# ScalarE's square-root functions asked for ahead of the norms, sigmoid and silu made from exp in the sparse attention, and the two tiles' norm steps interleaved at three places

## The reference, cut to what matters

```python
def rms_norm(x, g):        # ahead of both parts of each hybrid layer, and at its end
    y = xf * lax.rsqrt(jnp.mean(xf * xf, axis=-1, keepdims=True) + NORM_EPS)
    return (y * g.astype(jnp.float32)).astype(x.dtype)
def layer_norm(x, g, b):   # l0, l1, l2, l3 in the kernel
    mu = jnp.mean(xf, axis=-1, keepdims=True)
    var = jnp.mean(jnp.square(xf - mu), axis=-1, keepdims=True)
    return ((xf - mu) * lax.rsqrt(var + LN_EPS) * g + b).astype(x.dtype)
def compress(k, pe, w1, w2):
    ...
    return jax.nn.silu(blk @ w1) @ w2
gates = jax.nn.sigmoid(g_logits.astype(jnp.float32))   # in nsa_mixer
```

## Time and profile before

| what | value |
|---|---|
| median of 3 runs | 2278.53 us |
| lowest and highest run | 2272.89 and 2286.32 us |
| profiled execution, its own time | 2274.16 us |
| its span | 2272.4 us |
| PE, DVE, ACT busy share of the span | 94%, 70%, 58% |
| granted TensorE clock, mean | 0.976 |

### The profile page before, as it was taken

The page is one execution under the profiler, slowest core; times in us unless marked ns, Lnnn a source line. Parts: engine busy times, 40 slices in busy tenths (PEclk is TensorE's granted clock), DMA queues, the critical chain, the costliest instruction groups (busy, mean ns, idle before and its releaser), DMA issues.

```text
span 2272.4 us, 26136 instructions
## 1 busy us (share of the span) xinstructions
PE 2145.5 (94%) x10090; PEld 1727.6 (76%) x10090; DVE 1596.6 (70%) x1554; ACT 1324.1 (58%) x1378; POOL 20.4 (1%) x32
## 2 busy tenths in 40 slices
PE   8889999989999999998888999999999999999997
PEld 7667887767788788777667888788888877777675
DVE  4965555776555645566755555788888899999997
ACT  5454444645444443445644544576776788887886
POOL 0000000000000000000000000000000000000000
PEclk9989999999999999997899999999999999999998
DMA  7314553431655455432007555788998999999995
GB/s 263 139 47 153 185 185 131 167 121 68 250 183 183 150 185 185 164 138 75 1 19 272 211 207 183 272 341 348 342 363 331 367 362 421 392 421 375 421 389 217
DMA packets 74625, 524.29 MB, mean 231 GB/s; under 512 B 8736, under 2 KB 9184, under 8 KB 12160
## 3 DMA queue, kind: packets, MB, share of 16 engines
q1 hardware_dynamic: 71712, 511.64, 59.2%
q0 software_dynamic: 2784, 10.93, 1.4%
HBM read 521.48 MB, written 1.05 MB: 230 GB/s over the span
## 4 chain that ended last, share of the span: by engine, by line
PE 66%; DVE 19%; ACT 6%; issue 6%; DMA 3%; DVEq 0%; ACTq 0%; SPq 0%; POOLq 0%
PE psum L516 57%; DVE LO L507 10%; ACT HI L499 2%; DMA ring<-in_experts 2%; DVE AR L1556 1%; PE psum L1030 1%; PE psum L2406 1%; PE psum L1025 1%; ACT AR L845 1%; PE psum L2434 1%; PE psum L879 1%; PE psum L816 1%; PE psum L664 1%; PE psum L683 1%; PE psum L1943 1%
## 5 line engine op out<-in xcount | busy, mean ns | idle before, releaser
L507 DVE TENSOR_TENSOR LO<-ring,HI 128x2048 fp32r<-128x2048 f32 x379 | 850.8, 2259 | 398.9 <-ACT HI L499 393.2
L499 ACT ACTIVATE HI<-ring 128x2048 fp32r<-128x2048 f32 x379 | 712.7, 1887 | 350.8 <-PE psum L516 340.3
L516 PE MATMUL psum<-HI,XT 128*128 128x512 f32 (+1 forms) x3152 | 805.2, 394 | 22.4 <-issue 5.7
L516 PEld LDWEIGHTS psum<-HI,XT 128*128 128x128 f32 x3152 | 592.4, 191 | 165.4 <-DVE XT L699 10.9
L516 PE MATMUL psum<-LO,XT 128*128 128x512 f32 (+1 forms) x1856 | 507.2, 395 | 16.6 <-DVE LO L507 14.2
L516 PEld LDWEIGHTS psum<-LO,XT 128*128 128x128 f32 x1856 | 345.4, 190 | 112.5 <-DVE LO L507 44.3
L516 PE MATMUL psum<-HI,HTH 128*128 128x512 f32 x848 | 306.3, 402 | 6.9 <-DVE HTH L1082 6.9
L507 DVE TENSOR_TENSOR LO<-AR,HI 128x2048 fp32r<-128x2048 f32 x112 | 254.9, 2290 | 53.6 <-ACT HI L499 53.0
L499 ACT ACTIVATE HI<-AR 128x2048 fp32r<-128x2048 f32 x112 | 212.7, 1911 | 60.3 <-PE psum L516 57.2
L516 PE MATMUL psum<-LO,HTH 128*128 128x512 f32 x848 | 229.9, 393 | 0.0
L516 PE MATMUL psum<-HI,HTL 128*128 128x512 f32 x568 | 221.5, 390 | 0.0
(11 more groups left out here) (270 smaller groups left out, 1464.8 us busy)
## 6 DMA issues: line engine op xcount, KB each, us to landing
ring<-in_experts SPq DMA_DIRECT2D x224, 1024.0 KB, 6.6
ring<-in_dense SPq DMA_DIRECT2D x149, 1024.0 KB, 4.8
AR<-in_experts SPq DMA_DIRECT2D x112, 1024.0 KB, 6.5
bcs<-in_ln_g POOLq DMA_DIRECT2D x4, 512.0 KB, 4.6
bcs<-in_ln_b POOLq DMA_DIRECT2D x4, 512.0 KB, 5.1
bcs<-in_norm_g POOLq DMA_DIRECT2D x3, 512.0 KB, 3.9
cons<-in_cons POOLq DMA_DIRECT2D x1, 1317.0 KB, 8.0
X<-in_x SPq DMA_DIRECT2D x2, 512.0 KB, 4.0
```

The lines of the kernel that those rows point to most:

```text
L499: e.activation(HI[:, h:h + m], slot(u), ACT.Copy).then_inc(*high.up(u))
L507: e.tensor_tensor(LO[:, h:h + m], slot(u), HI[:, h:h + m].bitcast(F32), ALU.subtract).then_inc(*low.up(u))
L516: ins = e.matmul(out_ap, lhsT=a, rhs=b, start=start and n == 0, stop=stop and n == len(pairs) - 1)
```

## The change

`first_root` is a new ScalarE instruction: the square root of a constant into a spare column. It stands ahead of everything in layer 0, and ahead of the squares of `l1`, `l2` and `l3`. The functions of the norms are cut into their steps. In layer 0 both tiles' squares and sums come ahead of tile 0's split, and TensorE turns tile 1's rows ahead of the first product. In `l2` VectorE splits tile 0 only after tile 1's centred values. In `l3` both tiles' means, sums and centred values come ahead of both tiles' rows. In the sparse attention Sigmoid and Silu become Exp of the negated input on ScalarE, and VectorE adds one, takes the reciprocal and, for Silu, multiplies.

```diff
+        def first_root(e):
+            e.wait_ge(*v_done.of("eps"))
+            e.wait_ge(*a_order.last)
+            e.activation(sm(1, "root"), EPS[:, 0:1], ACT.Sqrt).then_inc(*a_done.up())
...
         def ln_stat(e, name, t):
+            if t == 0 and name != "l0":
+                first_root(e)
+            ln_squares(e, name, t)
+            ln_root(e, name, t)
...
             if l == 0:
-                idle_first(e, 10)
+                idle_first(e, 3)
             turn_rows(e, n1, 0, lambda k: ROWS[:, 0, tile(k)], rows_of(n1, 0), rest=l)
-            if l == 0:
-                idle_first(e, 18)
             def second_rows():
                 turn_rows(e, n1, 1, lambda k: ROWS[:, 1, tile(k)], rows_of(n1, 1), wait=l, rest=l, b=BA[0])
-                if l == 0:
-                    idle_first(e, 4)
-            cols_by_tile(e, ("raw", l, 0), ("qk", l, 0), BOTH, xr, between=second_rows)
+            if l == 0:
+                idle_first(e, 6)
+                second_rows()
+            cols_by_tile(e, ("raw", l, 0), ("qk", l, 0), BOTH, xr, between=second_rows if l else None)
...
+            if l == 0:
+                first_root(e)
             rms_stat(e, n1, 0, x_at)
+            if l == 0:
+                rms_squares(e, n1, 1, x_at)
             cols_hi(e, n1, 0)
             if l:
                 split_hi(e)
-            rms_stat(e, n1, 1, x_at)
+                rms_squares(e, n1, 1, x_at)
+            rms_root(e, n1, 1)
             if l == 0:
                 split_hi(e, AHEAD)
...
-                rms_apply(e, n1, t, ROWS, *vector(n1))
+                if t and l == 0:
+                    rms_rows(e, n1, 1, ROWS, *vector(n1))
+                else:
+                    rms_apply(e, n1, t, ROWS, *vector(n1))
                 if t == 0:
+                    if l == 0:
+                        rms_sum(e, n1, 1)
                     cols_lo(e, n1, 0)
...
-            e.wait_ge(*a_done.of("hid", kind))
+            e.wait_ge(*v_done.of("hid", kind))
...
                 e.activation(GT[:, t, :], banks.get("gates", 2, "turned")[:, t * 48:(t + 1) * 48],
-                             ACT.Sigmoid).then_inc(*(a_bank.up("gates", 2, "turned") if t
+                             ACT.Exp, scale=-1.0).then_inc(*(a_bank.up("gates", 2, "turned") if t
...
-                e.activation(hv, hv, ACT.Silu).then_inc(*a_done.up("hid", kind))
+                e.activation(sm(60, "hid").rearrange("p (g n) -> p g n", g=4), hv, ACT.Exp,
+                             scale=-1.0).then_inc(*a_done.up("hid", kind))
...
+        def one_over_one_more(e, x):
+            e.wait_ge(*v_order.last)
+            e.tensor_scalar(x, x, 1.0, None, ALU.add).then_inc(*v_done.up())
+            e.wait_ge(*v_order.last)
+            e.reciprocal(x, x).then_inc(*v_done.up())
+        def hidden_silu(e, kind):
+            hv = HID.rearrange("p (g n) -> p g n", g=4)[:, :, 0:15]
+            ex = sm(60, "hid")
+            e.wait_ge(*a_done.of("hid", kind))
+            one_over_one_more(e, ex)
+            e.wait_ge(*v_order.last)
+            e.tensor_tensor(hv, hv, ex.rearrange("p (g n) -> p g n", g=4),
+                            ALU.mult).then_inc(*v_done.up("hid", kind))
...
+            def gates():
+                e.wait_ge(*a_bank.of("gates", 2, "turned"))
+                one_over_one_more(e, A(16000, 96))
...
+            steps |= {1: gates, 3: lambda: hidden_silu(e, 0), 9: lambda: hidden_silu(e, 1),
...
-            ln_stat(e, "l3", 0)
-            ln_stat(e, "l3", 1)
+            first_root(e)
+            ln_squares(e, "l3", 0)
+            ln_squares(e, "l3", 1)
+            ln_root(e, "l3", 0)
+            ln_root(e, "l3", 1)
...
-                ln_apply(e, "l2", t, *vector("l2"), *vector("l2b"))
-                if t == 0:
+                ln_mean(e, "l2", t)
+                ln_center(e, t, *vector("l2"))
+                if t:
                     cols_lo(e, "l2", 0)
+                ln_sum(e, "l2", t)
+                ln_rows(e, "l2", t, *vector("l2b"))
             cols_lo(e, "l2", 1)
...
-                ln_apply(e, "l3", t, *vector("l3"), *vector("l3b"))
+                ln_mean(e, "l3", t)
+                if t:
+                    ln_sum(e, "l3", 0)
+                ln_center(e, t, *vector("l3"))
+            for t in range(2):
+                if t == 0:
+                    ln_sum(e, "l3", 1)
+                ln_rows(e, "l3", t, *vector("l3b"))
```

More of the change, by code:

```diff
@@ L702, in cols_lo, with rms_squares @@
                                 ALU.subtract).then_inc(*v_bank.up(name, "cols", t, k0))
+        def first_root(e):
+            e.wait_ge(*v_done.of("eps"))
+            e.wait_ge(*a_order.last)
+            e.activation(sm(1, "root"), EPS[:, 0:1], ACT.Sqrt).then_inc(*a_done.up())
         def rms_stat(e, name, t, x_at):
-            st, mv, r = sm(2, "st", t), sm(2, "mv", t), sm(1, "r", t)
+            rms_squares(e, name, t, x_at)
+            rms_root(e, name, t)
+        def rms_squares(e, name, t, x_at):
+            st = sm(2, "st", t)
             for nh in range(2):
@@ L713, in rms_stat, with rms_root @@
                              accum_out=st[:, nh:nh + 1]).then_inc(*a_done.up(name, "sq", t, nh))
+        def rms_root(e, name, t):
+            mv, r = sm(2, "mv", t), sm(1, "r", t)
             e.wait_ge(*v_done.of(name, "sum", t))
@@ L719, in rms_apply, with rms_sum @@
         def rms_apply(e, name, t, dst, gv, g_at):
-            st, mv, r = sm(2, "st", t), sm(2, "mv", t), sm(1, "r", t)
+            rms_sum(e, name, t)
+            rms_rows(e, name, t, dst, gv, g_at)
+        def rms_sum(e, name, t):
+            st, mv = sm(2, "st", t), sm(2, "mv", t)
             e.wait_ge(*a_done.of(name, "sq", t, 1))
@@ L724, in rms_apply, with rms_rows @@
                             ALU.add).then_inc(*v_done.up(name, "sum", t))
+        def rms_rows(e, name, t, dst, gv, g_at):
+            r = sm(1, "r", t)
             e.wait_ge(*a_done.of(name, "root", t))
@@ L735, in ln_stat, with ln_squares @@
         def ln_stat(e, name, t):
-            ss, mv, r = sm(2, "ss", t), sm(2, "mv", t), sm(1, "r", t)
+            if t == 0 and name != "l0":
+                first_root(e)
+            ln_squares(e, name, t)
+            ln_root(e, name, t)
+        def ln_squares(e, name, t):
+            ss, mv = sm(2, "ss", t), sm(2, "mv", t)
             for nh in range(2):
@@ L741, in ln_stat, with ln_root @@
                              accum_out=ss[:, nh:nh + 1]).then_inc(*a_done.up(name, "sq", t, nh))
+        def ln_root(e, name, t):
+            mv, r = sm(2, "mv", t), sm(1, "r", t)
             e.wait_ge(*v_done.of(name, "sum", t))
@@ L747, in ln_apply, with ln_mean @@
         def ln_apply(e, name, t, gv, g_at, bv, b_at):
-            st, ss, mv, r = sm(2, "st", t), sm(2, "ss", t), sm(2, "mv", t), sm(1, "r", t)
+            ln_mean(e, name, t)
+            ln_center(e, t, gv, g_at)
+            ln_sum(e, name, t)
+            ln_rows(e, name, t, bv, b_at)
+        def ln_mean(e, name, t):
+            st, mv = sm(2, "st", t), sm(2, "mv", t)
             e.wait_ge(*v_order.last)
@@ L753, in ln_apply, with ln_center, ln_sum @@
                             ALU.mult).then_inc(*v_done.up(name, "mean", t))
+        def ln_center(e, t, gv, g_at):
             e.wait_ge(*g_at)
             e.wait_ge(*v_order.last)
-            e.scalar_tensor_tensor(ROWS[:, t, :], X[:, t, :], mv[:, 1:2], gv, ALU.add,
+            e.scalar_tensor_tensor(ROWS[:, t, :], X[:, t, :], sm(2, "mv", t)[:, 1:2], gv, ALU.add,
                                    ALU.mult).then_inc(*v_done.up())
+        def ln_sum(e, name, t):
+            ss, mv = sm(2, "ss", t), sm(2, "mv", t)
             e.wait_ge(*a_done.of(name, "sq", t, 1))
@@ L761, in ln_apply, with ln_rows @@
                             ALU.add).then_inc(*v_done.up(name, "sum", t))
+        def ln_rows(e, name, t, bv, b_at):
+            r = sm(1, "r", t)
             e.wait_ge(*a_done.of(name, "root", t))
@@ L2203, in turn_c_vector @@
             e.reciprocal(l, l).then_inc(*v_done.up())
-            e.wait_ge(*a_bank.of("gates", 2, "turned"))
             e.wait_ge(*v_order.last)
@@ L2313, in sparse_vector @@
             steps = {2 * n: f for n, f in steps.items()}
-            steps |= {12: lambda: weigh_c_vector(e, 0), 14: lambda: turn_c_vector(e, 0),
+            steps |= {1: gates, 3: lambda: hidden_silu(e, 0), 9: lambda: hidden_silu(e, 1),
+                      12: lambda: weigh_c_vector(e, 0), 14: lambda: turn_c_vector(e, 0),
                       18: lambda: gather_c_vector(e, 0), 19: lambda: weigh_c_vector(e, 1),
@@ L2739, in vector_program @@
             e.wait_ge(*v_order.last)
-            e.memset(EPS[:, 1:2], 1e-6).then_inc(*v_done.up())
+            e.memset(EPS[:, 1:2], 1e-6).then_inc(*v_done.up("eps"))
             hybrid_vector(e, 0, lambda t, nh: None)
```

## The result

The changed kernel takes 2263.64 us (median of 13 runs, 2258.96 to 2271.4), the kernel before, run beside it, 2276.24 (13 runs, 2269.47 to 2288.87). The ratio is 0.9941, with an interval from 0.9925 to 0.9957: 13.4 us less, between 9.8 and 17.1. The profiled execution took 2260.03 with a span of 2258.2, which is 14.2 less than the span before. The page shows 22 loads of ScalarE's functions instead of 28. First the chain of waits of the kernel after, which answers to the earlier trace rows: TensorE's share grows by 2 points, ScalarE's and DMA's shrink by 1 each.

A forecast was written before the change was run, and what follows sets the result against it. TensorE holds two thirds of the chain; the change touches where it stands still for unfinished norms. Terms 4.0 + 0.7 + 0.6 + 0 + 1.9 + 2.8 + 2.3 = 12.3 us give 2261.9 or 2266.2, middle 2264, range 2256 to 2272.

The forecast's parts named there:

- start, order and fillers, with banks: Layer 0: tile 1's products start at 20.6 to 21.0 instead of 24.75, 4.0 us, plus 0.7 us from banks.
- banks within it: Layer 0, third unit: its products use long-empty banks, so the 0.73 stop at 31.22 goes; 0.7 us.
- l1: Norm l1: the load at 953.13 goes, but TensorE had only 0.51 us idle there; 0.6 us.
- sparse, keys' path: Sparse attention, keys: product 0.95 us later, absorbed by 1.14 us of TensorE idle at 1061.45; together 0.
- sparse, values: Sparse attention, values: two loads in a row on ScalarE go, the weight split at 1084.16 starts at 1082.25; 1.9 us.
- l2: Norm l2: tile 1's transposes start 2.2 us sooner, plus 0.6 for TensorE not falling to half clock; 2.8 us.
- l3: Norm l3, the end: tile 1's residuals directly follow tile 0's centred values, rows end at 2267.65 instead of 2269.93; 2.3 us.
- The cold TensorE: Rival at the start: fewer fillers delay the full clock, losing 3 to 4 us of 4.7, total 8.5; chance 0.20.
- VectorE's dear work: Rival in sparse attention: reciprocals cost twice the slope, sparse gains +0.5 in all, total 10.5 or less; chance 0.15.
- Loads dearer than their rows: Rival: a drain makes four loads on the path give 1.38 more each, gain 17.8; chance 0.04.
- The loads moved as written: Answers the rival that the root's set lacks Square, each norm loading twice more; gain 7, chance 0.03.
- The half clock did not stay on: Answers the slower rival: TensorE at half clock for most of the first stage, 2290 us; chance 0.03.

The follow-up runs named there:

- p_banks: Kernel before with the PSUM bank count moved on by two ahead of layer 0's second projection group; 2277.52 us, ratio 0.9997.
- a_again: Kernel after, unchanged, profiled a second time; 2260.75 us (4 runs), ratio 0.993 to the kernel before.
- p_start: Kernel before with only the start changed: root load ahead, new order, 3 and 6 fillers; 2271.1 us, ratio 0.996.
- b_again: Kernel before, unchanged, profiled a second time; 2280.23 us, ratio 1.0015.
- p_exp: Kernel before with only the sparse attention changed, exp and VectorE work for sigmoid and silu; 2276.48 us, ratio 0.999.
- a_keysilu: Kernel after with the keys' hidden layer back on ScalarE's Silu, the values' still on exp; 2266.45 us, ratio 0.9944.
- p_order: Kernel before with only the order of l2 and l3 changed, loads left in front of the roots; 2275.22 us, ratio 0.9968.
- p_loads: Kernel before with only the square-root loads ahead (first_root at the start, l1, l2, l3); 2270.45 us, ratio 0.9967.
- a_nofill: Kernel after without any filler products at the start (0 in both places); 2269.99 us, ratio 0.9957 to the kernel before.
- four part kernels: p_loads, p_start, p_exp and p_order, each one part of the change on the kernel before; ratios 0.9967, 0.996, 0.999, 0.9968.
- a_gfirst: Kernel after with norm_g's transfer issued ahead of the second tile of x; 2261.26 us, ratio 0.9929 to the kernel before.

## Why the prediction was right

With fourteen traces, the terms can be read at their own places and averaged over kernels that share the code there. The start goes to the split of VectorE that stands at 38.98 in the kernel before. The sparse part goes from the split at 1047.66 to that at 1084.16 (the earlier trace rows has the latter); all distances are differences of row starts.

| term | predicted | measured | from |
|---|---|---|---|
| start, order and fillers, with banks | 4.7 | 5.4 | 38.6 (4 traces without) less 33.2 (5 traces with the change's start) |
| banks within it | 0.7 | 0.9 | `p_banks` |
| l1 | 0.6 | 0.8 | lead of 5.74 at the residual, 6.56 at the next split |
| sparse, keys' path | 0 | -0.7 | 13.79 to 14.47 at the transposes |
| sparse, values | 1.9 | 1.5 to 1.9 | 9.59 to 8.13, and 7.73 in `a_again`, which like before has full clock there |
| sparse, whole region | 1.9 | 3.6 | 37.7 (6 traces) less 34.1 (6 traces) |
| l2 | 2.8 | 2.4 to 2.7 | 16.99 to 14.61; 2.7 with the work up to the next split |
| l3 | 2.3 | 2.05 | 13.08 to 11.03 |
| sum | 12.3 | about 14 | the ratio gives 13.4 (9.8 to 17.1) |

**The start** is the largest term, and was 0.7 too small. The four traces without the change stand between 38.3 and 39.0, the five with it between 32.8 and 34.1, so the gain is beyond the scatter of either. The scatter has two sources: in the kernels without the change the first product (16.05 to 16.75) goes with the time at which the fillers reach the full rate (9.4 to 11.4), and in the five with it the product starts 6.4 to 6.8 us behind the rows that waited for norm_g. The step that was off is "Tile 0's products took 6.1 us": they take 5.6 (14.34 to 19.90 in `p_start`), since nothing waits for VectorE's low halves any more. The first product at 14.34 instead of 14.5 to 14.9 and the banks' 0.2 add to it. In the first trace norm_g came 1.1 us later than I had it from the earlier trace rows, and hid that.

**The keys' product** comes 1.0 later, priced 0.95; the reciprocals take 0.53 and 0.75, priced 0.51 and 0.73, so the line through the earlier trace rows holds up to 96 columns. The 1.14 us of idle at 1061.45 did take up delay, as I had written, and is gone. What my sum lacked is the clock. TensorE's work from the keys' product to its next free moment takes 4.37 us in the kernel before and 5.18 in the kernel after, and 1.01 + 0.81 - 1.14 gives the 0.68 that is lost. The last scores ahead of the idle ran at the full rate before (timeline of the kernel before):

```profile
1059.67 0.65 PE L816 MATMUL psum<-AR 128*128 128x256 f32 x2
```

The same two take 1.17 in the kernel after (row 1054.73). Nor was the load at 1055.79 off the path. In the kernel before, the keys' rotation on VectorE waited for ScalarE's small copy of weights at 1059.60, behind the exps that this load held up. Without the load that copy is only 0.34 us later behind the split (1053.50 in the kernel after), although the product is 1.01 later, and the turned keys too are only 0.34 later.

**The region** gained more than both its steps. With both hidden layers on Silu, the six traces have 36.3 to 39.6 us; with both on exp, 33.5 to 34.6: no overlap. The windows from the second split to the third show why. First `b_again`, one of the long ones, then `a_again`:

```profile
1072.41:1089.28 16.87, 16.29 (x79) 12.54 (x78) 8.50 (x15) 10.63 (x26) 0.00 (x0) 0.73 0.01 2
```

```profile
1064.37:1076.80 12.43, 10.98 (x72) 8.31 (x70) 9.45 (x18) 8.07 (x23) 0.00 (x0) 0.99 0.02 4
```

In the kernel before at 1.00 this stretch takes 14.29, at 0.99 in `a_again` 12.43: 1.86 of gain at the same clock, which is the predicted 1.9. The rest is clock: three of six Silu traces pay 2.6 more here, the exp traces at most 0.7 (`p_exp`, at 0.86; the first trace of after pays 0.4 at 0.84), and `a_keysilu` (16.53 at a clock of 0.72) pays too. Ahead of it, the exp traces are 0.8 quicker to the second split on the mean (21.3 for 22.1), although the keys' product is later. That too goes with the clock. In the seven traces with the keys on Silu, TensorE has a granted clock of 0.57 to 0.65 from the first split to the transposes, stands idle 1.0 to 1.7 us in front of them, and runs at 0.54 to 0.68 behind them, so that the second split comes 7.2 to 8.9 us later. In the seven with the keys on exp it is 0.50, no idle, then 0.74 to 0.93, and 6.6 to 7.15 us. I had no such term. In clock and idle ahead of the second split the two groups do not overlap in 14 traces (in the whole time from first to second split they do: `p_start`, with Silu, takes 20.95). Behind it their clocks overlap: `before`, `p_order` and `p_loads` have Silu and full clock. Why the keys' path should move the clock was not isolated.

**l2, l3** came out as worked, 0.1 to 0.4 and 0.25 less. At l2, of the 2.38 at the routing 1.94 is the earlier transposes, which I had at 2.2, and 0.44 the clock behind them, which I had at 0.6. My reason for the clock isn't borne out: the idle in front shrank to 1.12 and not below 1 us, and `p_loads` runs these transposes at a granted clock of 1.00 behind an idle of 2.68, `p_exp` at 0.84 behind 2.33, the kernel before at 0.55 behind 2.33. Both places repeat well: in the seven traces that have the change there, the routing is at 14.60 or 14.61 and l3 takes 11.03 or 11.04. At l3 the change orders both roots behind both sums, so tile 0's rows start at 7.65 behind the first residual, where I had 7.55, and the two pairs of rows take 3.38 instead of 3.28. The lesson of `p_order` is that my sum there silently used two gains, which alone are worth 0.8 (order) and 1.1 (load).

**The rivals.** The cold TensorE did not come (products of 0.25 from the first) and is sized by `a_nofill`, 1.4 us. The margin was thin: the passes reach the full rate within 0.3 us of the first product in two of the six traces with three and six fillers, the first of the kernel after among them, and 0.9 to 1.8 us ahead in the other four. VectorE's dear work is refuted by its rows. Loads dearer than their rows: `p_loads` shows 1.14 at l3 for a load of 1.28, and the load starts 0.08 us behind ScalarE's last work there, where I had 0.04. The Trainium skill ("ScalarE: Activation LUTs", What ACT_TABLE_LOAD costs) has some 2.66 for a switch with its drain; no run here shows it, and the sum of 17.8 by it lies outside the interval. The loads moved as written. The half clock did not stay on.

**The level** was the other half of the forecast. I took 2264 as a middle between 2262 and 2266 because executions differ; it is 0.4 from the median of after, but the two medians of before (2278.53 and 2276.24) alone differ by 2.3, so being that near was luck. The four part kernels show the same: `p_order` gains 2.0 us at its two places and 7 by its ratio (3 to 11), `p_loads` 2.4 at its places and 7.5 (3 to 12). The shares of the parts by ratio, 7.5 + 9 + 2.3 + 7.3, come to twice the whole, and only the start's load is in two of them, so this is no overlap of the parts.

The runs' own clocks say where most of the excess lies. In the 85 runs of the kernel before that stand beside the experiments, time and mean granted clock go together (correlation -0.88, some 1.8 us less for each 0.001 more). Measured from that line, at equal clock, `p_loads` (mean clock 0.975 against 0.972) is 1.0 us shorter and `p_order` (0.974) 1.0 longer, neither clear of zero by twice its error of 0.6 and 0.9; `p_start` is 5.2 shorter, `p_exp` 0.4, and the 13 runs of the kernel after (0.974) are 10.2 shorter, with an error of 0.5. Lines fitted to each round alone move the four parts by at most 0.3. So some 3 of the 13.4 us go with a higher mean clock. An edit can itself move the clock, as in the sparse part, so this isn't proof of chance. But the 12.3 that I worked out held no such gain beyond 0.6 at l2, and that it lies within 1.1 of 13.4 is in part luck too.

## What to carry to other kernels

Price a change at its own place, from a landmark just ahead of it to one just behind, in several traces of kernels that share the code there; a lead that wanders in code that is the same says how far a total can be trusted, here 4 us and once 14. Where every run has its mean clock, compare the kernels at equal clock too. A load of functions is worth nearly its row where ScalarE's next result is waited for (1.14 at l3) and less where something else holds the next step (0.4 at l2), and an order that puts both tiles behind the load makes it dearer. An idle gap takes up a delay only if the work in front of it keeps its speed: here that work fell to half clock and 0.7 us came through.

## What was not expected of the hardware

Two traces of one kernel differ by 10.2 us of 2272 in span, with a mean granted clock of 0.976 and 0.969; in one stretch of 30 us it is 1.00 against 0.77. The landing of one 512 KB transfer at the start took 5.9, 7.0, 6.0 and 5.2 us from its issue (before, after, `a_again`, `a_gfirst`); with the change's start the products followed the rows that waited for it, but not in `a_gfirst`. TensorE ran its products at the full rate behind 18 filler passes and 16 transposes, but without any filler the first eight products took 3.53 us for 2.1.
